# A decoder step on one core: scatter-adds split over two DRAM tables, and the order of the start and of the end changed with them

## The reference

```python
x = x + gate1 * mixer(rmsnorm(x) * (1 + scale1) + shift1)
h = rmsnorm(x) * (1 + scale2) + shift2
# 64 experts, top 8 per token by sigmoid scores with group limits; D_EXPERT = 256
hg = einsum('nd,edf->nef', h, e_gate);  hu = einsum('nd,edf->nef', h, e_up)
act = silu(hg) * hu * gates[:, :, None]
routed = einsum('nef,efd->nd', act, e_down)
x = x + gate2 * (routed + shared(h));  y = rmsnorm(x) * final_g
```

## Time and profile before

| | before |
|---|---|
| median of 3 runs | 984.89 us |
| the profiled execution | 984.89 us, its span 983.1 us |
| PE busy | 861.4 us (88%) |
| DVE busy | 464.1 us (47%) |
| ACT busy | 272.3 us (28%) |
| POOL busy | 171.7 us (17%) |
| DMA | 305.55 MB, mean 311 GB/s |
| mean granted TensorE clock | 0.949 |

### The profile page before, as it was taken

How to read it: one execution, slowest core, us unless ns; L and a number is a source line. 1 busy time by engine, 2 the same in 40 slices (tenths; PEclk the granted TensorE clock), 3 DMA queues, 4 the chain that set the end, 5 groups by cost and what they waited for, 6 DMA issues and landing times.

```text
span 983.1 us, 20818 instructions
## 1 busy us (share of the span) xinstructions
PE 861.4 (88%) x7579; PEld 627.8 (64%) x7579; DVE 464.1 (47%) x1252; ACT 272.3 (28%) x521; POOL 171.7 (17%) x178
## 2 busy tenths in 40 slices
PE   3699999999998999999988889888897798798880
PEld 2699999999997987346554555544554454464450
DVE  2656889899967564523222222322322322232124
ACT  4544444443284220012112121211211212121122
POOL 2010000000000001022223222322222322322211
PEclk9799999999999979999999999999999999899895
DMA  9974558879876259679999999999999999999932
GB/s 331 302 238 149 176 176 292 270 255 308 278 270 224 82 214 372 230 288 339 369 384 402 388 392 389 407 390 394 392 397 380 400 388 396 401 377 390 385 122 93
DMA packets 99843, 305.55 MB, mean 311 GB/s; under 512 B 11459, under 2 KB 51459, under 8 KB 74796
## 3 DMA queue, kind: packets, MB, share of 16 engines
q1 hardware_dynamic: 87275, 281.63, 75.6%
q0 software_dynamic: 12016, 21.78, 8.5%
q10 hardware_dynamic: 499, 1.40, 0.4%
HBM read 301.86 MB, written 21.97 MB: 329 GB/s over the span
## 4 chain that ended last, share of the span: by engine, by line
PE 52%; DMA 36%; issue 6%; DVE 4%; ACT 1%; SPq 0%; POOL 0%; POOLq 0%; ACTq 0%; DVEq 0%
PE psum L765 26%; DMA wexp<-in_e_up 24%; PE psum L1040 12%; DMA y_even<-mT,scatter_row 10%; PE psum L769 3%; PE psum L784 3%; PE psum L1079 2%; PE psum L952 2%; DMA wexp<-in_ada_w 1%; PE psum L1007 1%; DVE wexp_r L1467 1%; PE psum L1042 1%; PE psum L1037 1%; DVE x_sb L2028 0%; PE psum L1084 0%
## 5 line engine op out<-in xcount | busy, mean ns | idle before, releaser
L765 PE MATMUL psum<-xn_r,wexp_r 128*128 128x264 f32 x1024 | 192.5, 288 | 2.4 <-DVE wexp_r L1467 2.4
L1040 PE MATMUL psum<-wexp,mid 128*128 128x512 f32 x304 | 150.2, 643 | 28.5 <-DMA wexp<-in_e_up 27.5
L765 PEld LDWEIGHTS psum<-xn_r,wexp_r 128*128 128x128 f32 x1024 | 161.1, 191 | 3.5 <-DVE wexp_r L1467 2.7
L765 PE MATMUL psum<-hT_r,wexp_r 128*128 128x264 f32 x512 | 146.1, 285 | 0.0
L689 POOL DMA_INDIRECT y_even<-mT,scatter_row x64 | 92.9, 1452 | 272.4 <-ACT mT L1386 106.5
L1040 PEld LDWEIGHTS psum<-wexp,mid 128*128 128x128 f32 x304 | 59.4, 206 | 95.7 <-issue 94.2
L1467 DVE TENSOR_TENSOR wexp_r<-wexp,wexp_r 128x1024 fp32r<-128x1024 f32 x88 | 106.4, 1217 | 25.5 <-ACT wexp_r L1218 25.3
L1885 DVE SCALAR_TENSOR_TENSOR hT<-psum,gcol,hT 128x256 f32<-128x256 f32 (+1 forms) x64 | 26.4, 413 | 192.7 <-ACT hT L1374 189.0
L1218 ACT ACTIVATE wexp_r<-wexp 128x1024 fp32r<-128x1024 f32 x88 | 92.2, 1054 | 51.2 <-PE psum L765 41.5
L765 PEld LDWEIGHTS psum<-hT_r,wexp_r 128*128 128x128 f32 x512 | 97.6, 191 | 0.1
L765 PE MATMUL psum<-wexp_r 128*128 128x264 f32 (+2 forms) x576 | 82.6, 284 | 2.7 <-DVE mT_r L1683 2.2
(11 more groups left out here) (294 smaller groups left out, 1095.0 us busy)
## 6 DMA issues: line engine op xcount, KB each, us to landing
wexp<-in_e_gate SPq DMA_DIRECT2D x64, 1024.0 KB
wexp<-in_e_up SPq DMA_DIRECT2D x64, 1024.0 KB
wexp<-in_e_down SPq DMA_DIRECT2D x64, 1024.0 KB
wexp<-in_w_in SPq DMA_DIRECT2D x32, 1024.0 KB, 6.1
mid<-in_ada_w SPq DMA_DIRECT2D x8, 2048.0 KB, 9.6
wexp<-in_ada_w SPq DMA_DIRECT2D x4, 2048.0 KB, 20.4
wexp<-in_w_branch SPq DMA_DIRECT2D x8, 1024.0 KB, 6.1
wexp<-in_w_out SPq DMA_DIRECT2D x4, 1024.0 KB, 5.7
```

What stands on the lines that cost most here:

```text
L765: last = mm(out, a[x], b[y], start=start and x == y == 0, stop=stop and x == 1)
L1040: last = mm(psum[:, j % 2, :].rearrange("p (a f) -> p a f", a=2), x[:, k, :], w[:, k], start=(k == 0), stop=(k == KT - 1))
```

## The change

A second table, `y_odd`, takes the scatters of jobs 1 and 3 of each round; `y_even` keeps those of jobs 0 and 2. Each table has its own count `scattered[j % 2]`, and a scatter waits only for those of its own table. On POOL the scatter now comes ahead of the gather. At the end the even table is loaded as soon as its last scatter is done, and DVE adds it to x; the odd table follows after all scatters and the extra-pass check, with tiles 0 and 1 on DVE and the sample tile on POOL. The final norm goes over the tiles in the order 0, 1, 2. Both tables are zeroed. The table load for the root stands ahead of the extra-pass check on ACT. At the start `prow0` and the hT transposes come ahead of `ada(0)` on PE, and the copy of `prow0` ahead of the norm on DVE.

```diff
-    out = ["cT", ("ada", 0)] + [("hT", k) for k in range(KT)]
-    out += ["prow0", ("ada", 1), ("modT", 0), ...
+    out = ["cT", "prow0"] + [("hT", k) for k in range(KT)]
+    out += [("ada", 0), ("ada", 1), ("modT", 0), ...
...
+        scattered = [sem(f"scattered{b}") for b in range(2)]
-        fin_y = wexp[:, 1, 0:3 * D].rearrange("p (t d) -> p t d", t=3)
+        fin_y = wexp[:, 1, :].rearrange("p (a t d) -> p a t d", a=2, t=3)
...
-            for table in (y_even,):
+            for table in (y_even, y_odd):
...
+            sp.wait_ge(S["down_done"], 2 * (NE - 2))
+            sp.wait_ge(scattered[0], 16 * (NE // 2))
+            for t, (t0, n) in enumerate(TILES):
+                sp.dma_start(fin_y[0:n, 0, t], y_even[t0:t0 + n]).then_inc(S["even_load"], 16)
             sp.wait_ge(S["down_done"], 2 * NE)
             extra_passes(sp, extra)
             sp.wait_ge(S["moe_done"], 1)
-            sp.wait_ge(S["scattered"], 16 * NE)
-            for t in FINAL_ORDER:
+            for t in (2, 0, 1):
                 t0, n = TILES[t]
-                sp.dma_start(fin_y[0:n, t], y_even[t0:t0 + n]).then_inc(fin_ld[t], 16)
+                sp.dma_start(fin_y[0:n, 1, t], y_odd[t0:t0 + n]).then_inc(fin_ld[t], 16)
...
             def scatter(i, j):
                 pool.wait_ge(S["scatter_row_ready"], e + 1)
-                need(pool, S["scattered"], 16 * e)
+                need(pool, scattered[j % 2], 16 * (2 * i + j // 2))
...
-                g.indirect_dma_start(out=y_even, ...
+                g.indirect_dma_start(out=(y_even, y_odd)[j % 2], ...
...
             def body(i, first=False, last=False):
                 for j in range(UNROLL):
+                    if not (first and j == 0):
+                        scatter(i if j else i - 1, (j - 1) % UNROLL)
                     if not last:
                         gather(i + 1, j)
-                    if not (first and j == 0):
-                        scatter(i if j else i - 1, (j - 1) % UNROLL)
...
+            pool.wait_ge(scattered[0], 16 * (NE // 2))
+            pool.wait_ge(scattered[1], 16 * (NE // 2))
-            extra_passes(pool, extra, all_scattered)
+            extra_passes(pool, extra)
             pool.sem_inc(S["moe_done"], 1)
-            all_scattered()
+            t, n = 2, NS
+            pool.wait_ge(fin_ld[t], 16)
+            link(g.tensor_tensor(out=fin_y[0:n, 1, t], in0=fin_y[0:n, 1, t], in1=rows_of(3, t, n, 0, D), op=ALU.mult))
+            pool.wait_ge(S["even_taken"], 3)
+            g.tensor_tensor(out=x_sb[0:n, t, :], in0=x_sb[0:n, t, :], in1=fin_y[0:n, 1, t], op=ALU.add).then_inc(S["fin_samples"], 1)
...
-            ada(0)
+            pe.wait_ge(S["ld_prow"], 7 * 16)
+            out = claim("prow0")
...
             pe.wait_ge(S["x_norm"], 3)
             for k in range(KT):
                 out = claim(("hT", k))
...
-            pe.wait_ge(S["ld_prow"], 7 * 16)
-            out = claim("prow0")
...
+            ada(0)
             ada(1)
...
-                need(ac, S["scattered"], 16 * (e - 1))
+                need(ac, scattered[j % 2], 16 * (2 * i + j // 2))
...
+            ve.wait_ge(S["even_load"], 3 * 16)
+            for t, (t0, n) in enumerate(TILES):
+                link(V.tensor_tensor(fin_y[0:n, 0, t], fin_y[0:n, 0, t], rows_of(3, t, n, 0, D), ALU.mult))
+                V.tensor_tensor(x_sb[0:n, t, :], x_sb[0:n, t, :], fin_y[0:n, 0, t], ALU.add).then_inc(S["even_taken"], 1)
             extra_passes(ve, extra, shift_smaller)
-            for t in FINAL_ORDER:
+            for t in range(2):
                 ve.wait_ge(fin_ld[t], 16)
-                link(V.tensor_tensor(fin_y[0:n, t], fin_y[0:n, t], rows_of(3, t, n, 0, D), ALU.mult))
-                V.tensor_tensor(x_sb[0:n, t, :], x_sb[0:n, t, :], fin_y[0:n, t], ALU.add).then_inc(S["fin_red"], 1)
+                link(V.tensor_tensor(fin_y[0:n, 1, t], fin_y[0:n, 1, t], rows_of(3, t, n, 0, D), ALU.mult))
+                ve.wait_ge(S["even_taken"], t + 1)
+                V.tensor_tensor(x_sb[0:n, t, :], x_sb[0:n, t, :], fin_y[0:n, 1, t], ALU.add).then_inc(S["fin_red"], 1)
             ve.wait_ge(S["ld_fin"], 16)
-            for m, t in enumerate(FINAL_ORDER):
+            for t, (t0, n) in enumerate(TILES):
```

More of the change, by code:

```diff
@@ L63, in jobs_of_mixer @@
 def jobs_of_mixer():
-    out = ["cT", ("ada", 0)] + [("hT", k) for k in range(KT)]
-    out += ["prow0", ("ada", 1), ("modT", 0), ("ada", 2), ("modT", 1), ("modT", 2), ("ada", 3), ("modT", 3)]
+    out = ["cT", "prow0"] + [("hT", k) for k in range(KT)]
+    out += [("ada", 0), ("ada", 1), ("modT", 0), ("ada", 2), ("modT", 1), ("modT", 2), ("ada", 3), ("modT", 3)]
     for kind, j in BLOCKS:
@@ L664, in _ @@
             pool.wait_ge(S["h2_stored"], 3 * 16)
-            pool.wait_ge(S["tables_zero"], 2 * 16)
+            pool.wait_ge(S["tables_zero"], 4 * 16)
             last_token = pool.alloc_register("last_token")
@@ L688, in scatter @@
                 n = rows_used(i, j)
-                g.indirect_dma_start(out=y_even, out_offset=bass.IndirectOffsetOnAxis(ap=scatter_row[0:n, j, :].bitcast(mybir.dt.uint32), axis=0),
+                g.indirect_dma_start(out=(y_even, y_odd)[j % 2], out_offset=bass.IndirectOffsetOnAxis(ap=scatter_row[0:n, j, :].bitcast(mybir.dt.uint32), axis=0),
                                      in_=y_rows[0:n, j % 2, :], in_offset=None,
-                                     bounds_check=last_token, oob_is_err=False, compute_op=ALU.add).then_inc(S["scattered"], 16)
+                                     bounds_check=last_token, oob_is_err=False, compute_op=ALU.add).then_inc(scattered[j % 2], 16)
             await_full(pool, ("h2T", MIX_ORDER[-1], 1))
@@ L725, in extra @@
                 pool.sem_inc(S["dma_may_go"], 1)
-                g.indirect_dma_start(out=y_even, out_offset=bass.IndirectOffsetOnAxis(ap=idx[:, 0, 0:1].bitcast(mybir.dt.uint32), axis=0),
+                g.indirect_dma_start(out=y_odd, out_offset=bass.IndirectOffsetOnAxis(ap=idx[:, 0, 0:1].bitcast(mybir.dt.uint32), axis=0),
                                      in_=y_rows[:, 0, :], in_offset=None,
@@ L793, in turn_mod @@
                 full(last, ("modT", j))
-            ada(0)
+            pe.wait_ge(S["ld_prow"], 7 * 16)
+            out = claim("prow0")
+            for c in range(CT):
+                last = turn(out[:, c * NPROW:(c + 1) * NPROW], prow[:, c * P:(c + 1) * P], NPROW)
+            full(last, "prow0")
             pe.wait_ge(S["x_norm"], 3)
@@ L801, in _ @@
                 full(last, ("hT", k))
-            pe.wait_ge(S["ld_prow"], 7 * 16)
-            out = claim("prow0")
-            for c in range(CT):
-                last = turn(out[:, c * NPROW:(c + 1) * NPROW], prow[:, c * P:(c + 1) * P], NPROW)
-            full(last, "prow0")
+            ada(0)
             ada(1)
@@ L1415, in extra @@
                 F(actT[:, 0], psum[:, 2, 0:2 * P].rearrange("p (h c) -> p h c", h=2), ACT.Copy).then_inc(S["x_actT"], 1)
+            F(sqrt_first[:], epsc[:], ACT.Sqrt)
             extra_passes(ac, extra)
[L1418 to L1421, removed]
+            for t, (t0, n) in enumerate(TILES):
+                if t == 2:
+                    ac.wait_ge(S["fin_samples"], 1)
+                else:
+                    ac.wait_ge(S["fin_red"], t + 1)
                 link(F(xn[0:n, t, :], x_sb[0:n, t, :], ACT.Square, accum_out=st[0:n, t, 0:1]))
@@ L1503, in h_samples @@
                 V.tensor_tensor(hT[:, k, SEQ:TOK], hT[:, k, SEQ:TOK], S1[:, k, 0:NS], ALU.add).then_inc(S["h_ready"], 1)
+            b = await_full(ve, "prow0")
+            free(V.tensor_copy(prm[:].rearrange("p c r -> p (c r)"), b[:, 0:CT * NPROW]), "prow0")
             ve.wait_ge(S["x_sq"], 1)
@@ L1510, in _ @@
             ada_out(0)
-            b = await_full(ve, "prow0")
-            free(V.tensor_copy(prm[:].rearrange("p c r -> p (c r)"), b[:, 0:CT * NPROW]), "prow0")
             ada_out(1)
```

20 lines of the change are left out of this document (8 added, 12 removed).

## The result

The changed kernel takes 993.02 us (median of 9 runs, 992.67 to 995.78), the kernel before in the same comparison 986.84 us (9 runs, 982.7 to 989.2). The ratio is 1.0069 [1.0051, 1.0087]: slower by 6.8 us, with 5.0 to 8.6 inside the interval. The forecast was 987.4 us with a range of 982.5 to 993.0; the time lies at the range's upper edge, on the far side of it, and beyond rival A (991.2).

What follows compares the result with a forecast made beforehand. The prediction took bytes (DMA) to bound the kernel from 440 to 930 us, with a chain of scatters, load and DVE work at the end. 984.89 + 0.6 (parts 3 to 5) + 1.9 (part 6) = 987.4 us, range 982.5 to 993.

Steps and rivals of the forecast that it cites:

- rival A: Final arithmetic: POOL's two sample operations hold DVE for 5.7 us instead of 1.9, total 991.2 us; chance 0.24.
- Part 7: Start: prow0 and hT ahead of ada(0) cost 0, from -0.5 to +1 us, lateness hidden behind ada(3)'s load.
- A price for an idle load: Start: if a load lay idle behind the late ada(3), it would cost those 3 us.
- Part 6: End: two sample operations on POOL hold DVE up, +1.9 us (2 x 0.94), between 0 and 5.7.
- Parts 3 and 4: Tail: overlapping scatters let the even table load 7.05 us earlier; DVE's final arithmetic starts 4.0 us earlier.
- Rival C: Tail: both scatters go through one queue, no overlap, even load 3.1 us later than summed, total 990.5 us; chance 0.12.
- Part 3: End of the scatter chain: with two tables scatter 62 ends 3.2 us earlier and scatter 63 nearly 6.
- Part 5: Final arithmetic: ten DVE operations of 1.22 us instead of six; the end moves +0.4 to +0.8 us, taken as +0.6.
- Part 1: Expert stage: two scatter chains in two tables move packets against each other and take none away, 0.
- rival B: Expert stage: serial scatters hold it, two in flight free it, 8.4 us gained, total 979.0 us; chance 0.10.
- Part 2: POOL order: scatter ahead of gather costs 0, as gathered rows are wanted three jobs later, some 25 us.
- Part 8: Zeroing y_odd: two more issues on SP at 320 to 329 us, at a DMA share of 0.05, cost 0.

Runs made afterwards that it cites:

- s3: Kernel before with ada(0) moved behind the hT batches and prow0, prow0 not ahead of hT, its copy behind the norm: 985.19 us, ratio 0.9986.
- s1: Kernel before with only the changed kernel's start (prow0 and hT ahead of ada(0), copy of prow0 ahead of the norm): 989.45 us, ratio 1.0040.
- s5: s1 with DVE's copy of the parameter rows behind the norm of x instead of ahead of it: 986.80 us, ratio 1.0004 to the kernel before.
- s6: s1 with the seven parameter-row loads issued right behind the loads of x on ACT's queue: 987.03 us, ratio 0.9999 to the kernel before.
- s2: Changed kernel with the old order of the start: 989.95 us, ratio 1.0047 to the kernel before.
- t3: s2 with each scatter waiting for all scatters before it, of both tables: 990.00 us, ratio 1.0040 to the kernel before.
- t2: s2 with the first square root behind the extra-pass check on ACT, as before the change: 990.16 us, ratio 1.0048 to the kernel before.
- o1: Kernel before with only the scatter put ahead of the gather in POOL's list: 983.01 us, ratio 0.9978.
- o2: The same kernel as o1, timed a second time: 983.04 us, ratio 0.9981 to the kernel before.
- b1: s2 with PE adding the two tables into PSUM, samples on DVE, first root behind the check, samples tile first: 994.23 us, ratio 1.0068.
- t1: s2 with the sample tile's two odd-table operations on DVE instead of POOL: 987.72 us, ratio 1.0030 to the kernel before.

## Why the prediction was wrong, point by point

**Part 7, the start, is the step that failed.** It said: if the rows land after 14.6 us, "some 4 us of it would still be hidden behind the load of ada(3)", and "ada(2) and ada(3) still stand ahead of them in the queue". The cover in the first was mis-sized, and so was the lateness. s3 is the same order of the start without the rows in front: its transposes begin at 14.87 and its ada(3) at 33.10. In after they begin at 21.24 and 37.80. So 6.4 us of lateness came out as 4.7, and the wait for ada(3)'s load covers 1.7 us, not some 4. (s1, 20.71 and 37.00, gives 5.8, 3.9 and 1.9.) And the lateness was not only that of the rows' landing, 17.99 against 14.6: DVE's copy of the rows ahead of the norm put as much again on top, 17.99 to 21.24. The second held only until 28 us: w_in's loads came not 3 to 6 but 12 us later, and the queue ran nearly dry. I had left the rows' landing open, gave its lateness a cover, and did not follow what is left once the cover is used up: from the mixer's first product on PE has next to no idle time, and the lateness stays. s1 (+3.9 us), s3 (transposes first are free) and s5 and s6 (the loss gone with 3 us of lateness less) show it from both sides. The sign to look for, ada(3) later than 33 us, was named and came; it had no chance of its own. A price for an idle load was named too ("it would cost those 3 us"). That the hole of 3.4 us is close to the loss of 3.9 looks like a hit, but in the traces the products wait for PE's own chain and not for the hole.

**Part 6, the samples on POOL, was the right mechanism with the term too small.** 1.9 us were taken from 2 x 0.94; it was 2 x 2.01 = 4.0 (3.24 instead of 1.23 us). POOL's operation begins at 970.70, while DVE's multiply runs until 971.49, and ends at 973.68: 2.19 us after DVE's end. DVE's next began at 971.52, behind POOL, and runs 2.01 us longer than its twins. The second pair repeats it: POOL ends at 982.87, 2.18 us behind DVE's 980.69. So POOL's own work is 2.2 us; the rows that I had priced it by, a fill and a select, were of other operations. The Trainium skill has this case (SBUF — State Buffer, "SBUF: two separate sides"): whoever begins first keeps the shared pair for a whole instruction. The trace agrees, both ways round, with 2.0 us. The Trainium skill's 2.6 cycles per element (GPSIMD Engine Reference, "Elementwise — side-by-side cycle accounting") had given an estimated 2.2 us, which is what the trace shows (2.19 and 2.18). The sum by it, 989.9, stood beside the forecast, which went by the shorter row.

**Parts 3 and 4, scatters and final load: right.** Relative to PE's end the even load was forecast at 4.2 us and came at 4.1; DVE was forecast to start at 9.1 and did at 9.5 (9.6 in s2), 3.5 us earlier than before, forecast 4.0. Part 3 gave the overlap in flight 3.2 us at scatter 62; t3 puts it at 2.3 to 3.0 there, and at 1.7 to 2.4 at DVE's start. Rival C did not come: the even load is issued 20.0 to 20.9 us behind job 60's product where the scatters overlap, and 23.0 behind it in t3, where they don't.

**Part 5, the arithmetic.** Ten operations, as forecast. The table reload on ACT was not seen. It follows from the first root standing ahead of a branch, and t2 shows that it cost nearly nothing. By positions s2's tail adds up: DVE starts 3.5 us earlier, four operations more are 4.9, two holds 4.0, the wait for the root 0.5, the smaller last store about -0.7, in sum +5.2; the tails differ by 5.2 (32.7 and 27.5). The ratio of s2 says 4.6.

**Part 1, two chains in the stage: 0, right.** s2 was ahead in the middle and lost it again. Its scatter 16 is issued at 557.92 us where the kernel before has 569.49, its scatter 40 at 772.65 against 772.38, its scatter 60 at 946.63 against 945.09. All five kernels with two chains issue scatter 16 at 556.6 to 561.1 us, the nine with one chain at 568.9 to 578.9, t3 among them, so the lead is that of the overlap; at scatter 60 nothing of it is left (942.7 to 949.5 against 942.2 to 951.3). That is what a stage bound by bytes would show; rival B did not come.

**Part 2, scatter ahead of gather: predicted 0, measured -2 us** (o1, o2). The reason given, that the gather has time, holds in the changed kernel, where PE never waits for gathered rows. It doesn't hold with one chain of scatters (o1, o2 and t3: 17.4 to 21.8 us of such waits), and there the waits cost nothing. That the scatter gains anything was not weighed.

**Part 8, the zeroing: 0, right.** The two stores are issued at 326.1 and 328.5 us, and nobody waits for them.

In sum the forecast had +2.5 us, all of it at the end. By positions the end is +5.2 (the hold alone 2.1 more than forecast), the start +3.9 and the order -2, together 7.1 where the whole measures 6.8. So close a fit is in part luck. s2 holds everything but the start, so by this sum it should be +3.2, and it measures +4.6 (2.8 to 6.5).

## What to carry to other kernels

Before a transfer is called hidden, find when it lands; where no row shows it, the step that will wait for it gets a price and a chance, not a cover. Then follow the late step to the work from which on the engine has no idle time: here PE came 5 us late to the mixer's first product and kept 4 of them to the end, while the hole in the DMA queue, which was easier to see, held nothing up in the traces. Count a stretch from a mark that the change doesn't move: from PE's end, a wait for the last weights looked like a shorter tail. And don't move a small operation from VectorE to GpSimd beside VectorE operations with two inputs: 2.4 us of work moved away cost 4.0 us of standing.

## What the runs showed of the hardware that I had not expected

Loads of a few kB landed late while four loads of 2 MB were under way from another queue: of the rows, issued from 5.4 to 7.2 us, the last was there only at 17.99, some 10.7 us after its issue, while the same rows issued from 1.9 us on landed by 14.2, and as the very first by 8.65, with x then late in their place. No run takes the large loads away, so that they are the reason isn't shown.

TensorE's pace at the start is not set by the order of the work alone. The 24 transposes of x take 4.25 us in the kernel before and 6.63 in o1, with the same work ahead of them; 6.63 in the changed kernel, behind 13 us with 0.65 us of work. The granted clock reads 1.00 in all these stretches. b1's sum, behind 10.17 us of idling, ran at a granted clock of 0.50 (1.2 GHz).

Scatter-adds into two tables do run side by side: scatter 61 is issued 6.1 us behind scatter 60 in s2, t1, t2 and the changed kernel, and 9.2 us behind it in t3, where it waits for it.
